# Reordering ScalarE's work around an MLP, and computing attention's v token by token

## The reference

```python
# first block, its last part
hn = rms_norm(h, norm_mlp_g)
up = relu(hn @ w_mlp_up)                 # 1024 -> 4096
h = h + (up * up) @ w_mlp_down           # 4096 -> 1024
# second block (after an ffn of its own)
z = rmsnorm(h, mix_pre_g) @ w_in         # q, k, v of attention (3 x 512), then 1920 columns for rwkv
q, k = rope(q) / 8, rope(k)              # 8 heads of 64
y_att = sum over 3 dilated windows of softmax(q k) v, merged by their log sums, then normed by head
y_rwkv = bidirectional rwkv7(z[1536:])   # 8 heads of 64, decays, keys grown by the inverse decay
h = h + rmsnorm(concat(y_att, y_rwkv) @ w_out, mix_post_g)
```

## Time and profile before

| | us |
|---|---|
| median of three runs | 1195.75 |
| profiled execution | 1201.01 |
| its span | 1197.9 |
| TensorE matmuls busy | 1164.8 (97%) |
| GpSimd busy | 897.3 (75%) |
| ScalarE busy | 629.3 (53%) |
| VectorE busy | 553.0 (46%) |
| span and mean rate of transfers | 192.77 MB, 161 GB/s |

### The profile page before, as it was taken

The page is one execution under the profiler, slowest core; times in us unless marked ns, Lnnn a source line. Parts: engine busy times, 40 slices in busy tenths (PEclk is TensorE's granted clock), DMA queues, the critical chain, the costliest instruction groups (busy, mean ns, idle before and its releaser), DMA issues.

```text
span 1197.9 us, 25527 instructions
## 1 busy us (share of the span) xinstructions
PE 1164.8 (97%) x10770; PEld 1093.6 (91%) x10770; DVE 553.0 (46%) x973; ACT 629.3 (53%) x1008; POOL 897.3 (75%) x689
## 2 busy tenths in 40 slices
PE   6999999999999999999999999899999998999998
PEld 6999989999997899998999999799989987999997
DVE  2553476452652222223653323557876545333334
ACT  5676576647644445444744444679442316444443
POOL 5987665876986999998799999587710025999994
PEclk9999999999999999999999999999999999999999
DMA  7655444655576566665566666555500024666663
GB/s 249 187 182 164 135 124 132 197 165 152 183 216 191 170 182 190 185 185 176 160 192 182 188 189 182 197 163 181 155 3 4 4 92 141 191 181 191 185 185 105
DMA packets 53776, 192.77 MB, mean 161 GB/s; under 512 B 6304, under 2 KB 7328, under 8 KB 53280
## 3 DMA queue, kind: packets, MB, share of 16 engines
q1 hardware_dynamic: 50640, 183.00, 50.3%
q10 hardware_dynamic: 3024, 8.16, 2.0%
HBM read 189.03 MB, written 1.05 MB: 159 GB/s over the span
## 4 chain that ended last, share of the span: by engine, by line
PE 91%; DVE 4%; ACT 2%; DMA 2%; issue 1%; ACTq 0%; POOL 0%; DVEq 0%
PE product L524 19%; PE product L526 19%; PE product L525 19%; PE bank L590 7%; PE bank L592 7%; PE bank L591 7%; PE bank L1082 3%; PE product L1082 3%; DMA raw_ring<-in_w_in 1%; PE product L1029 1%; PE bank L629 1%; PE bank L524 1%; PE product L1009 1%; PE bank L525 1%; PE bank L526 1%
## 5 line engine op out<-in xcount | busy, mean ns | idle before, releaser
L500 POOL TENSOR_TENSOR weight_lo<-raw_ring,weight_hi 128x512 fp32r<-128x512 f32 x684 | 892.5, 1336 | 282.6 <-ACT weight_hi L2284 261.6
L2284 ACT ACTIVATE weight_hi<-raw_ring 128x1024 fp32r<-128x1024 f32 x338 | 357.0, 1060 | 407.8 <-DMA raw_ring<-in_ffn_gu 108.6
L524 PE MATMUL product<-operand_B_hi,weight_hi 128*128 128x256 f32 x1104 | 311.8, 282 | 1.7 <-POOL weight_lo L500 1.5
L526 PE MATMUL product<-operand_B_hi,weight_lo 128*128 128x256 f32 x1104 | 311.2, 282 | 0.0
L525 PE MATMUL product<-operand_B_lo,weight_hi 128*128 128x256 f32 x1104 | 310.8, 282 | 0.0
L524 PE MATMUL product<-operand_A_hi,weight_hi 128*128 128x256 f32 x840 | 242.1, 288 | 11.2 <-DVE weight_lo L1410 11.2
L526 PE MATMUL product<-operand_A_hi,weight_lo 128*128 128x256 f32 x840 | 238.5, 284 | 0.0
L525 PE MATMUL product<-operand_A_lo,weight_hi 128*128 128x256 f32 x840 | 238.2, 284 | 0.0
L524 PEld LDWEIGHTS product<-operand_B_hi,weight_hi 128*128 128x128 f32 x1104 | 208.0, 188 | 4.9 <-POOL weight_lo L500 2.1
L525 PEld LDWEIGHTS product<-operand_B_lo,weight_hi 128*128 128x128 f32 x1104 | 207.9, 188 | 3.1
L526 PEld LDWEIGHTS product<-operand_B_hi,weight_lo 128*128 128x128 f32 x1104 | 207.9, 188 | 0.0
(11 more groups left out here) (367 smaller groups left out, 1402.6 us busy)
## 6 DMA issues: line engine op xcount, KB each, us to landing
raw_ring<-in_w_in SPq DMA_DIRECT2D x107, 512.0 KB, 3.6
raw_ring<-in_ffn_gu SPq DMA_DIRECT2D x88, 512.0 KB, 3.6
raw_ring<-in_ffn_down SPq DMA_DIRECT2D x44, 512.0 KB, 3.6
raw_ring<-in_w_mlp_up SPq DMA_DIRECT2D x32, 512.0 KB, 4.3
raw_ring<-in_w_mlp_down SPq DMA_DIRECT2D x32, 512.0 KB, 4.3
raw_ring<-in_w_out SPq DMA_DIRECT2D x16, 512.0 KB, 4.3
raw_ring<-in_w_branch_c SPq DMA_DIRECT2D x8, 512.0 KB, 3.6
raw_ring<-in_w_branch_a SPq DMA_DIRECT2D x8, 512.0 KB, 3.6
```

The source lines that it names most:

```text
L500: last = k.nc.gpsimd.tensor_tensor(k.wlo[:, slot, part], k.raw[:, slot, part], k.whi[:, slot, part].bitcast(F32), ALU.subtract)
L524: mm(ps, w_hi, op.hi[:, b, :], start=b == 0, stop=False)
L526: return mm(ps, w_lo, op.hi[:, b, :], start=False, stop=b == blocks - 1)
L2284: k.nc.scalar.activation(k.whi[:, slot, 0:w], k.raw[:, slot, 0:w], ACT.Copy).then_inc(k.s["hi_ready"], 1)
```

## The change

Four edits. (1) Ahead of the MLP the high parts of tiles up 2, down 0 and up 3 move: the first behind the sixth operand high, the others behind the eighth, and the four row sums go into the loop behind up 4 to up 7. (2) In the MLP's loop ScalarE makes relu j first, and the high part behind it; the high of hidden j+2 comes behind the high part at down j (hidden 0 and 1 behind relu 1 and 2). VectorE's reciprocal goes behind up 12. (3) v of attention becomes a segment of its own, `att_v`: four tiles of 256 input rows x 512 columns, token-major, summed in the two banks that later hold scores and probabilities, copied by ScalarE with a scale per token. That scale comes from two transposes of `rs` and a copy of two columns by VectorE. The eight transposes and VectorE's four evacuations are gone; the first scores wait for the first copy, the first probabilities for the second. (4) VectorE makes the rotations of q and of half of k ahead of the grown keys.

```diff
 # plan and buffers
-    p.seg("qkv", "w_in_2", 0, 12, "hn_mix")
+    p.seg("qk", "w_in_2", 0, 8, "hn_mix")
+    p.seg("att_v", "w_att_v", 0, 4, "hn_mix", by_token=True)
...
+    k.value_bank = [k.score_bank, k.prob_bank]
...
-        self.rs_col = s[:, 0:2]
+        self.rs_col = s[:, 610:612]
 # TensorE
+            for ch in range(NCH):
+                last = k.nc.tensor.transpose(k.bank[1][:, ch * P:(ch + 1) * P], k.rs[:, ch * P:(ch + 1) * P], k.ident[:])
+            last.then_inc(s["rs_turned"], 1)
...
+            pe.wait_ge(s["rs_turned"], 2)
...
-    dense(k, pe, "qkv", after=behind_qkv)
-
-    def values_by_token():
-
-        for ch in range(NCH):
-            for b in range(AB):
-                if ch == 0 and b in (0, AB - 1):
-                    pe.wait_ge(s["evacuated"], k.segs["qkv"].slot + (11 if b == 0 else 12))
-                last = k.nc.tensor.transpose(k.slots[ch][:, b * P:(b + 1) * P],
-                                             k.qkv[:, 8 + b, ch * P:(ch + 1) * P], k.ident[:])
-            last.then_inc(s["vt_tr"], 1)
+    dense(k, pe, "qk", after=behind_qk)
+
+    def values_by_token(i):
+
+        seg, op = k.segs["att_v"], k.made["hn_mix"]
+        t = seg.start + i
+        slot = t % WRING
+        pe.wait_ge(s["lo_ready"], t + 1)
+        if i == 0:
+            pe.wait_ge(s["evacuated"], k.segs["qk"].slot + 6)
+        for m in range(NCH):
+            for part in range(2):
+                b, cols = 2 * i + part, slice(512 * part, 512 * part + 512)
+                hi, lo = (x[:, b, m * P:(m + 1) * P] for x in (op.hi, op.lo))
+                ps = k.value_bank[m][:]
+                mm(ps, hi, k.whi[:, slot, cols], start=b == 0, stop=False)
+                mm(ps, lo, k.whi[:, slot, cols], start=False, stop=False)
+                last = mm(ps, hi, k.wlo[:, slot, cols], start=False, stop=b == KB - 1)
+            if i == 3 and m == 0:
+                last.then_inc(s["vt_mm"], 1)
+        last.then_inc(s["tiles_used"], 1)
+
+    for i in range(4):
+        values_by_token(i)
+        behind_qk(8 + i)
...
+        else:
+            pe.wait_ge(s["vt_ev"], 1)
...
+        else:
+            pe.wait_ge(s["vt_ev"], 2)
...
-    pe.wait_ge(s["evacuated"], k.segs["qkv"].slot + 9)
+    pe.wait_ge(s["evacuated"], k.segs["qk"].slot + 8)
     attention(0)
-    values_by_token()
     pe.wait_ge(s["cbaq_made"], 1)
     pe.wait_ge(s["cb_made"], 1)
     first_products(0)
-    pe.wait_ge(s["vt_ev"], 2)
     first_products(1)
 # VectorE
+    def mlp_inverse():
...
             if j:
                 low_of_hidden(m, j - 1)
+            if j == 12:
+                mlp_inverse()
...
+    def norm_columns():
+
+        v.wait_ge(s["rs_turned"], 1)
+        nv.tensor_copy(c.rs_col, k.bank[1][:, 0:T:P]).then_inc(s["rs_turned"], 1)
...
     for i in range(12):
-        vector_evacuate(k, v, "qkv", rotated_in_part if i < 8 else plain(k.qkv), i, i + 1)
+        if i < 8:
+            vector_evacuate(k, v, "qk", rotated_in_part, i, i + 1)
         if i == 1:
+            norm_columns()
             kk_floor()
...
         elif i == 9:
-            grown_keys()
-        elif i == 10:
             rope(0, 0, 4)
             rope(1, 0, 2)
+            grown_keys()
     rope(1, 2, 2)
 # ScalarE
-    highs_of_turned(OUT_P, "hn_mlp", lambda b: col(k, "norm_mlp_g", b), lambda: None)
-    for i, (m, half) in enumerate(BY_FEATURES):
-        row_squares(part(k.x_tok, m, half), c.ss[:, 2 * m + half:2 * m + half + 1])
-    scalar_segment(k, act, "out", None, KB - AFTER, KB)
+    highs_of_turned(OUT_P, "hn_mlp", lambda b: col(k, "norm_mlp_g", b),
+                    lambda: scalar_segment(k, act, "out", None, KB - AFTER, KB - AFTER + 1))
+    scalar_segment(k, act, "out", None, KB - AFTER + 1, KB)
...
+    mlp_ahead = {m.tile[step] for step in m.order[:-AFTER]}
+
+    def mlp_high(j):
+        act.wait_ge(s["evacuated"], m.slot["up", j] + 1)
+        high_of_hidden(m, j)
+
+    high_part(k, act, m.tile["up", 0])
     for kind, j in m.order:
         t = m.tile[kind, j]
-        if (kind, j) not in m.order[-AFTER:]:
-            high_part(k, act, t)
         if kind == "up":
...
             f(k.pre[:, j % RING, :], k.product[n][:, 0:T], ACT.Relu).then_inc(s["act_out"], 1)
+            if j in (1, 2):
+                mlp_high(j - 1)
             if j:
-                act.wait_ge(s["evacuated"], m.slot["up", j - 1] + 1)
-                high_of_hidden(m, j - 1)
-            if j == HIDDEN - 1:
-                act.wait_ge(s["evacuated"], n + 1)
-                high_of_hidden(m, j)
+                high_part(k, act, t)
+            if 4 <= j < 8:
+                token_m, half = BY_FEATURES[j - 4]
+                row_squares(part(k.x_tok, token_m, half), c.ss[:, 2 * token_m + half:2 * token_m + half + 1])
+        else:
+            if t in mlp_ahead:
+                high_part(k, act, t)
+            if j + 2 < HIDDEN:
+                mlp_high(j + 2)
...
     for i in range(12):
-        scalar_segment(k, act, "qkv", None, i, i + 1)
+        if i < 8:
+            scalar_segment(k, act, "qk", None, i, i + 1)
+        elif i < 11:
+            scalar_segment(k, act, "att_v", None, i - 8, i - 7)
...
-    for ch in range(NCH):
-        act.wait_ge(s["vt_tr"], ch + 1)
-        f(k.att_v[:, ch, :], k.slots[ch][:], ACT.Copy).then_inc(s["vt_ev"], 1)
+    act.wait_ge(s["rs_turned"], 2)
+    for m in range(NCH):
+        if m == 0:
+            act.wait_ge(s["vt_mm"], 1)
+        else:
+            act.wait_ge(s["tiles_used"], values.start + 4)
+        f(k.att_v[:, m, :], k.value_bank[m][:], ACT.Copy, scale=c.rs_col[:, m:m + 1]).then_inc(s["vt_ev"], 1)
+    scalar_segment(k, act, "att_v", None, 3, 4)
```

More of the change, by code:

```diff
@@ L241 @@
     "l_ex decay_exp r_scaled wt_made bonus_in bonus_mm q_swap k_swap rope_ev "
-    "vt_tr vt_ev s_mm s_ev s_red s_exp p_tr p_ev o_mm o_ev o_sq o_sqrt o_fin o_tr "
+    "vt_mm rs_turned vt_ev s_mm s_ev s_red s_exp p_tr p_ev o_mm o_ev o_sq o_sqrt o_fin o_tr "
     "v_tok_mm v_tok_ev kka cb_made cbaq_made y_att_ev prod_mm nt_ev nt_in qb_ev ac_ev qc_ev ct_ev bt_ev "
@@ L311, in allocate @@
     uses["hn"] = k.segs["gate_b"].start + 8
-    uses["hn_mix"] = k.segs["qkv"].start + 12
+    uses["hn_mix"] = k.segs["att_v"].start + 4
     last_use = {}
@@ L376, in allocate @@
     k.upad = region(3840, 15, T + 2)
-    k.qkv = region(7712, 12)
+    k.qk = region(7712, 8)
     k.gout = region(3072, 4)
@@ L468, in sync_program @@
 def sync_program(k, sp, a, out):
-    qkv = k.segs["qkv"]
+    qk = k.segs["qk"]
     sp.dma_start(k.x[:, 0:4, :], a["x"][:, 0:4, :]).then_inc(k.s["x_in"], 16)
@@ L475, in sync_program @@
         for what in range(2):
-            if t == qkv.start + 4 * what + 10:
-                sp.wait_ge(k.s["evacuated"], qkv.slot + 4 * what + 4)
+            if t == qk.start + 4 * what + 10:
+                sp.wait_ge(k.s["evacuated"], qk.slot + 4 * what + 4)
                 if what:
@@ L949, in tensor_program, with behind_qk @@
     pe.wait_ge(s["late_in"], 128)
-    def behind_qkv(i):
+    def behind_qk(i):
         if i == 0:
@@ L1007, in scores @@
             pe.wait_ge(s["s_ev"], h)
+        else:
+            pe.wait_ge(s["vt_ev"], 1)
         for it in range(NCH):
-            last = mm(k.score_bank[:, it * T:(it + 1) * T], k.qkv[q:q + 64, h // 2, it * P:(it + 1) * P],
-                      k.qkv[q:q + 64, 4 + h // 2, :], start=True, stop=True)
+            last = mm(k.score_bank[:, it * T:(it + 1) * T], k.qk[q:q + 64, h // 2, it * P:(it + 1) * P],
+                      k.qk[q:q + 64, 4 + h // 2, :], start=True, stop=True)
         last.then_inc(s["s_mm"], 1)
@@ L1712, in vector_program @@
     lows_of_turned("hn_mlp", lambda b: col(k, "norm_mlp_g", b))
[L1713 to L1719, removed]
+    def mlp_inverse():
+        v.wait_ge(s["tok_sq"], 4)
+        st.do(nv.tensor_tensor(c.ms, c.ss[:, 0:4:2], c.ss[:, 1:4:2], ALU.add))
+        st.settle()
+        st.do(nv.tensor_scalar(c.ms, c.ms, 1.0 / D, EPS, ALU.mult, ALU.add))
+        st.settle()
+        st.do(nv.reciprocal(c.inv_sq, c.ms))
+        st.settle()
     hid_done = [0]
@@ L1975, in rotated_in_part @@
         what, b = i // 4, i % 4
-        st.do(nv.tensor_tensor(k.qkv[:, i, :], product, k.pre[:, 0, :], ALU.mult))
+        st.do(nv.tensor_tensor(k.qk[:, i, :], product, k.pre[:, 0, :], ALU.mult))
         nv.tensor_tensor(k.by_sine[what][:, b, :], product, k.pre[:, 1, :], ALU.mult).then_inc(s["evacuated"], 1)
@@ L1982, in rope @@
         v.wait_ge(s["k_swap" if what else "q_swap"], 64)
-        x = k.qkv[:, 4 * what + first:4 * what + first + n, :]
+        x = k.qk[:, 4 * what + first:4 * what + first + n, :]
         st.settle()
@@ L2749, in scalar_program @@
                   ACT.Copy).then_inc(s["v_tok_ev"], 1)
-    for ch in range(NCH):
-        act.wait_ge(s["vt_tr"], ch + 1)
-        f(k.att_v[:, ch, :], k.slots[ch][:], ACT.Copy).then_inc(s["vt_ev"], 1)
+    values = k.segs["att_v"]
+    act.wait_ge(s["rs_turned"], 2)
```

(2 more changed lines are left out.)

## The result

| | before | after |
|---|---|---|
| median, first comparison (5 runs each) | 1195.75 us | 1188.3 us (1187.07 to 1188.85) |
| profiled execution | 1201.01 | 1188.85 |
| its span | 1197.9 | 1187.0 |
| TensorE matmuls busy | 1164.8 | 1160.0 |

The changed kernel is faster, by 0.7%: ratio 0.9929, 95% interval 0.9905 to 0.9952, 7.45 us by the medians, against 8.05 forecast (1187.7) and a range of 1184.5 to 1193.5. The two profiles differ by more, 10.9 us of span, and that excess turned out to be the lesson of this case.

What follows compares the result with a forecast made beforehand. TensorE, with matmuls busy 97% of the span, was taken as the bound, so only less work or fewer stalls there help. Terms -5.8 - 1.5 - 0.75 = -8.05 us took the 1195.75 median to 1187.7, range 1184.5 to 1193.5.

Steps and rivals of the forecast that it cites:

- The MLP's start: Up 3 starts at 393.6 instead of 399.39, as two waits and a slow down 0 go: -5.8 us, bounds nothing and -5.8.
- I take it as gained: MLP's start: 1.6 us of the -5.8 is half clock in down 0, counted as gained because the stalls ahead go.
- Rival A: MLP's start: the clock falls all the same behind the transposes, leaving -6.4 us, 1189.3; chance 0.14.
- The MLP's loop: Row sums and later highs fit ScalarE's slack, hidden j+2 ready with 3.2 us to spare: term 0.
- The MLP's end: Relu 31 no longer stands behind a transfer, so the 1.48 us wait before down 30 goes: -1.5 us, bounds 0 and -1.7.
- what the transposes are worth: Attention: first products start 1.02 us earlier, at most 0.70 passes on; -0.75 us with the tiles' difference, bounds -1.3 and +1.1.
- the v tiles: Attention: 48 matmuls of 512 columns replace 96 of 256, 11.2 us against 11.95; taken as -0.3, bounds -0.5 and 0.
- The new wait: Attention: first scores wait for ScalarE's copy of v's first half, done 0.3 us in time: term 0, bounds 0 and +1.1.
- rival C: Attention: values come late behind a high part's transfer; +1.7 us, 1189.6, or 1190.5 if copies block the exponential; chance 0.07.
- E: MLP's start: nothing gained, given back where up 4's request waits for up 0; 1193.3; chance 0.06.
- B: MLP's start: GpSimd starts no earlier than about 387, low parts stay the bound, relus alone give 2.2 to 4; 1191.7; chance 0.11.
- D: MLP's loop: slower, every pair stalls once a transfer takes 7.5 us instead of 4.3; a microsecond beyond gives 1218; chance 0.04.

Runs made afterwards that it cites:

- transposes_double: Changed kernel with 16 dead transposes between attention's first scores and first products: 1191.49 us, ratio 0.9961 to the kernel before.
- att_only: Kernel before with only the diff's parts outside the MLP's edits (attention): 1195.40 us, ratio 1.0000 to the kernel before.
- att_again: Kernel before with attention's edits alone, measured a second time: 1193.66 us, ratio 0.9981 to the kernel before.
- old_loop: Changed kernel with the old order in the MLP's loop, early high part and sums in the loop kept: 1195.29 us, ratio 0.9992 to the kernel before.
- keys_first: Changed kernel with the grown keys ahead of the rotations again: 1189.76 us, ratio 0.9941 to the kernel before.
- transposes_back: Changed kernel with eight dead transposes of q between attention's first scores and first products: 1191.97 us, ratio 0.9958 to the kernel before.
- late_high: Changed kernel with the four row sums and three high parts back ahead of the MLP: 1192.10 us, ratio 0.9955 to the kernel before.
- mlp_again: Kernel before with the MLP's edits alone, measured a second time: 1193.68 us, ratio 0.9968 to the kernel before.
- mlp_only: Kernel before with the MLP's edits alone: 1192.37 us, ratio 0.9966 to the kernel before.
- after_third: Changed kernel, unaltered, measured a third time as a control: 1189.49 us, ratio 0.9948 to the kernel before.

## Why the prediction was right, and where it was not

**The MLP's start: mechanism right, size off.** Every time of the forecast chain was met within 0.3 us, once the 0.3 us by which this profile's lead came earlier are taken off: GpSimd 383.6 (forecast 384.0), relu 1 done 388.2 (388.6), hidden 0 low by 390.15 (390.7), up 3 at 393.25 (393.6). The term of -5.8 is exact for the two profiles (-5.83). But only 14.45 - 11.40 = 3.05 us of it are there against the other two profiles of the old MLP. The step that failed is "I take it as gained": the 1.6 us of the slow down 0, and 1.2 us of the wait ahead of it, were the luck of the profile read. Rival A, that the clock falls at the MLP's start all the same, did not happen: none of the ten profiles with relus ahead shows it there. What happened is that it falls elsewhere as often. The mean granted clock of all timed runs is 0.9973 for the kernel before (68 runs) and 0.9974, 0.9968 and 0.9970 in the changed kernel's three sets. 16 transposes stand ahead of the MLP's clock of 1.00 in those ten profiles, and in transposes_double the granted clock is 1.00 through sixteen in a row and behind them (846 to 858). The rule of the Trainium skill (TensorE: Matmul & The Clock Gate, "Part 4: PE-mode transpose") that transposes don't count as busy time for the clock in the same way had no effect that these runs show; they have no more than 2 us of transposes between dense matmuls, and test it no further.

**The MLP's loop: no gap, as forecast, but its pace is open.** After, an up tile and a down tile take 5.627 us together (mean of 27 each), before 5.654, with no wait in either; that is 0.8 us over the loop, and the forecast put it at nothing. All four profiles with the old order (before, att_only, att_again, old_loop) have the longer time. Of the ten with the new order eight have the shorter one, but keys_first and transposes_back have 5.654. So the order alone does not decide it, and whether it makes the shorter time likelier is open.

**The MLP's end: right, and a little large.** The wait before down 30 is gone. It was 1.48 us in the kernel before, 1.46 in att_only, 0.87 in att_again and 0.86 in old_loop, which all have the old order, so the term is -0.9 to -1.5. In the other profiles of the changed MLP 0 to 0.32 us is left in the last tiles, since hidden 31's low was forecast with 0.1 us to spare, and had 0.24 after.

**Attention: right in what the transposes are worth, low in the v tiles.** The two transposes added 0.22 us (0.25), and the v tiles take 11.44 instead of 11.95 us (-0.51, forecast -0.3). VectorE's first masked product started 2.56 us behind the scores, as forecast, instead of 3.32: -0.76, where the forecast let 0.70 pass on. That makes -1.05 us against -0.75. The profile after gained 0.2 us more in VectorE's chain, which is within the spread of that chain. The new wait (rival C) has its cover: 0.3 us here, but 0.47 us of wait in late_high, 0.56 in old_loop and 0.34 in transposes_double, where ScalarE's copies came later. That part of C is real and small.

**Sum.** The terms that repeat are -3.05, -0.9 to -1.5 and -1.05, so -5.0 to -5.6 us of span, and 0.7 us outside the span (below): -5.7 to -6.3. The three comparisons say -8.5 by ratio (7.45 by medians), -6.7 and -6.2. That my -8.05 was near the first is luck in part: 2.8 us of its largest term are not there in general, and what stood against that are terms that I had put at nothing or too low (the time outside the span, 0.3 us in attention, perhaps the loop's pace) and a first comparison that came out higher than the two later ones. About 1 us between the terms and the mean of the three is not explained. Two sums among the rivals are 0.2 us off by their own terms (C: 1187.7 + 1.7 = 1189.4, E: 1195.75 - 1.5 - 0.75 = 1193.5), and the room of ScalarE is in the earlier trace rows, not in rows 2; nothing hangs on either. Rivals B, D and E did not occur: up 2 to up 5 found their low parts, the loop had no gap in any profile, and nothing of the start was given back to the transfer of up 4.

## What to carry to other kernels

On an engine with one queue, put what is ready (a relu whose product is done) ahead of what waits for a transfer; moving only the transfer-bound work earlier shifts the wait to the next consumer (old_loop). The early high part was worth nothing without the loop's order, so two edits at one stall are measured together and apart. Before a stall is priced, see whether it is the same in a second execution: a wait that was longer in one profile than in two others, and the fall of the clock behind it, made half of the largest term here. In these runs a wait beside a fall of the clock had to be priced without the fall, since the fall turned up elsewhere once the wait was gone. And where a long stretch varies, look for the one instruction in it that waits: VectorE's wait for the transposes was 0.70 us in every profile with eight of them, while the stretch around it varied by more than a microsecond.

## What the runs showed of the hardware

Up to the end of TensorE's matmuls, an execution has none to two stretches at half clock (0.50, which is 1.2 GHz), of 3.4 us each, or 6.8 us in six of the nine that lie in the last block. In fourteen profiles the clock fell at the start of the MLP (2: before, behind waits of 1.54 and 2.23 us, and old_loop, behind one of 3.37), near 758 to 767 in the second block (5), in attention near 863 (2) and at the start of the last block (9, behind a wait of 1.69 us that all fourteen have); in mlp_again and transposes_double nowhere. No wait ahead of a fall was longer than 3.37 us; the shortest that stood alone ahead of one was 0.80 us (mlp_only, at 864), and a wait of 1.01 us in the same place left the clock at 1.00 (after_third). Between profiles of the same kernel the place changes, so what decides it is open. Through all 180 timed runs, a line for each kernel with a common slope gives 0.96 us of span for each 0.001 of mean granted clock; at a clock of 1 it puts the span at 1191.6 us before, 1183.9 to 1185.0 after, 1186.8 and 1187.0 with the MLP's edits, 1189.3 and 1189.8 with attention's, where the halves (4.7 and 2.1) add up to the whole (7.3) within 0.5 us.

The time outside the span was 1.8 us in every kernel with the separate array for v's weights, and on average 2.5 in the kernel before (68 runs) and 2.3 and 2.7 in mlp_only and mlp_again, where it lay anywhere from 1.8 to 3.8. Why is open; 0.7 us of the change's gain lies there.
